# Attention heads: banded score products ahead of the third transpose group, and outputs and that group's last two transposes in PSUM banks that the exponential has left

## What is computed

```
s_loc = jnp.where(allowed, q . k_band, NEG_INF)       # window heads: a band of +-128 latents
s_ctx = q . k_context                                 # and all 256 context keys
p = sink_softmax(concat([s_loc, s_ctx]), sink)
...
s = qn . kn + qr . kr                                 # latent heads: dense over 1280 keys
p = softmax(s * MLA_SCALE);  o = p . v
```

## Time and profile before

| | |
|---|---|
| three runs | 4216.95 us median (4215.39 to 4220.05) |
| profiled execution, its own time | 4216.5 us |
| its span, first to last instruction | 4214.8 us |
| PE busy | 4039.2 us, 96% of the span |
| PEld, DVE, ACT busy | 2856.4, 1892.8, 1076.1 us |
| PE's mean granted clock | 0.981 of full speed |
| PE in the chain that ended last | 82% of the span |
| L886 (latent scores), PE | 800 instructions, 349.7 us |
| L944 and L937 (outputs), L944 on PE | 2624 instructions, 157.3 us |

### The profile page before, as it was taken

One profiled execution on the slowest core, in us unless ns is written; L12 is line 12 of the kernel. 1 busy time (PEld: TensorE's weight loads), 2 busy tenths in 40 slices (PEclk: granted clock), 3 DMA queues, 4 the chain that ended last, 5 costly groups with the idle time before them and its releaser, 6 DMA issues.

```text
span 4214.8 us, 77861 instructions
## 1 busy us (share of the span) xinstructions
PE 4039.2 (96%) x31338; PEld 2856.4 (68%) x31338; DVE 1892.8 (45%) x4216; ACT 1076.1 (26%) x2469; POOL 253.7 (6%) x254
## 2 busy tenths in 40 slices
PE   8998999999999799999999999999999987999997
PEld 4555777655544588888887555777644446999996
DVE  2235666522235443333334444666533355444446
ACT  1225666400012111111111323666400120100103
POOL 0000000000000011111111000000000000101013
PEclk9999999999999899999999999999999998999998
DMA  6111000322244798888886211000222437999996
GB/s 209 55 51 50 16 16 16 118 73 70 70 156 183 268 284 267 266 267 266 266 266 203 85 63 56 16 16 16 71 45 45 156 115 233 328 330 327 330 324 223
DMA packets 568272, 655.05 MB, mean 155 GB/s; under 512 B 20404, under 2 KB 495172, under 8 KB 568088
## 3 DMA queue, kind: packets, MB, share of 16 engines
q1 hardware_dynamic: 548024, 603.17, 44.5%
q0 software_dynamic: 19488, 47.21, 4.5%
q10 hardware_dynamic: 576, 2.10, 0.1%
HBM read 581.03 MB, written 71.39 MB: 155 GB/s over the span
## 4 chain that ended last, share of the span: by engine, by line
PE 82%; DVE 3%; DMA 2%; issue 1%; DVEq 1%; ACT 1%; SPq 1%; POOL 0%; ACTq 0%; POOLq 0%
PE PS L714 34%; PE PS L1214 9%; PE PS L1243 9%; PE PS L718 8%; PE PS L886 6%; PE PS L1053 5%; PE PS L944 3%; PE PS L937 2%; PE PS L1237 1%; PE PS L857 1%; DVE arena L1617 1%; PE PS L854 1%; PE PS L729 1%; DVE arena L2061 1%; SPq L410 1%
## 5 line engine op out<-in xcount | busy, mean ns | idle before, releaser
L714 PE MATMUL PS<-arena 128*128 128x160 f32 (+4 forms) x7200 | 1773.2, 408 | 12.9 <-DVE arena L1617 5.1
L714 PEld LDWEIGHTS PS<-arena 128*128 128x128 f32 x7200 | 1143.5, 191 | 616.3 <-issue 559.0
L1617 DVE TENSOR_TENSOR arena<-arena,PS 128x256 f32<-128x256 f32 (+3 forms) x668 | 293.6, 448 | 1056.5 <-ACT arena L1586 566.8
L1617 DVE TENSOR_TENSOR arena<-arena 128x1024 f32<-128x1024 f32 (+9 forms) x826 | 590.3, 732 | 353.9 <-PE PS L714 234.1
L718 PEld LDWEIGHTS PS<-arena 128*128 128x128 f32 (+2 forms) x3218 | 379.0, 141 | 260.6 <-issue 148.0
L718 PE MATMUL PS<-arena 128*128 128x128 f32 (+2 forms) x3218 | 490.4, 280 | 45.0 <-DVE arena L1617 16.3
L1214 PE MATMUL PS<-arena 128*64 128x128 f32 x8192 | 457.2, 274 | 3.8 <-DVE arena L1617 1.7
L1214 PEld LDWEIGHTS PS<-arena 128*64 128x64 f32 x8192 | 452.6, 138 | 8.9 <-issue 3.9
L1243 PE MATMUL PS<-arena 128*64 128x256 f32 x3584 | 396.7, 382 | 1.8 <-DVE arena L1617 1.3
L1586 ACT ACTIVATE arena<-PS 128x160 f32<-128x160 f32 (+1 forms) x256 | 74.5, 291 | 1176.1 <-PE PS L714 654.3
L1243 PEld LDWEIGHTS PS<-arena 128*64 128x64 f32 x3584 | 274.3, 138 | 119.6 <-issue 12.4
(11 more groups left out here) (218 smaller groups left out, 2256.1 us busy)
## 6 DMA issues: line engine op xcount, KB each, us to landing
arena<-in_w_exp_gate SPq DMA_DIRECT2D x128, 1024.0 KB, 6.5
arena<-in_w_exp_up SPq DMA_DIRECT2D x128, 1024.0 KB, 9.0
arena<-in_w_exp_down SPq DMA_DIRECT2D x128, 1024.0 KB, 7.7
arena<-in_w_ada SPq DMA_DIRECT2D x24, 2048.0 KB, 20.5
arena<-in_w_in SPq DMA_DIRECT2D x32, 512.0 KB, 5.4
h_transposed<-arena SPq DMA_DIRECT2D x20, 512.0 KB, 4.4
x_mid<-arena SPq DMA_DIRECT2D x18, 512.0 KB, 3.5
moe_sum<-arena SPq DMA_DIRECT2D x18, 512.0 KB, 3.5
```

Of the source, the lines that this page charges most:

```text
L714: m = pe.matmul(o, lt, rh, start=start and i == 0, stop=stop and i == n - 1)
L1617: return dve.tensor_tensor(o, x, y, op)
```

## The change

It does six things.

1. `pair` on PE issues S_A2 of `n + 1`, W0, S_A0, then S_A1, W1, W2, then `banded`, then B0, B1, B2 (S_A2 and so on being the three score products of A). Before, W1 stood ahead of S_A1 and `banded` between B1 and B2.
2. B2 goes to the third bank of the set of A of `n + 1` and waits for that exponential (`pM`, 2N + 3) in place of the copy of B0.
3. `outputs` goes to the second bank of the same set, without the wait for the copies of bank 6. The first window product has no wait left; the latent products wait for the copy of B0 at the start, for that of B1 at key block 4 and for that of B2 at key block 8.
4. A1 no longer waits for `ob`; the score product S_B1 of `n + 1`, which writes the outputs' bank, waits for it instead.
5. W2 is copied by DVE, after the maxima of A and ahead of `divisors`, and no longer by ACT ahead of the exponential of A. The counts of `pt_a` and `pt_d` follow.
6. In a context head step the window scores of `n + 1` come ahead of B, and `outputs` waits for the exponential of A of `n + 1`.

```diff
+        def out_bank(n):
+
+            return score_set("A", n + 1) + 1
+
+        def turned(part, n, ci, blocks):
+
+            b = 6 + ci % 2 if part == "W" else 7 - ci % 2
+            if part == "B" and ci == 2:
+                b = score_set("A", n + 1) + 2
+            return PS[:, b, 0:blocks * P]
+
+        ON_DVE = {"A": (0,), "W": (0, 2), "B": (0,)}
...
-                        return [lambda: None, banded] if full else [context]
+                        return [banded] if full else [context]
...
+                        if i == 1 and part == "B" and later(N):
+                            pe.wait_ge(*s("ob", N))
...
-                        if part == "A" and ci == 0:
-                            if prev:
-                                pe.wait_ge(*s("pt_a", pa_count(l, *prev, last_copy(prev[0]))))
-                        elif part == "A" and ci == 1 or part == "W" and not full:
-                            if later(N):
+                        if not full:
+                            if part == "W" and later(N):
                                 pe.wait_ge(*s("ob", N))
-                        elif not full:
+                            if part == "B":
+                                pe.wait_ge(*s("pt_a", pa_count(l, lp, n, 1)))
+                        elif (part, ci) == ("A", 2):
+                            pe.wait_ge(*s("pt_d", pd_count(l, lp, n, 1)))
+                        elif (part, ci) == ("W", 0):
                             pe.wait_ge(*s("pt_a", pa_count(l, lp, n, 1)))
-                        elif ci == 2:
-                            pe.wait_ge(*s("pt_d", pd_count(l, lp, n, "AWB".index(part) + 1)))
-                        else:
-                            pe.wait_ge(*s("pt_a", pa_count(l, lp, n, ci + (1 if part == "W" else 3))))
+                        elif (part, ci) == ("W", 1):
+                            pe.wait_ge(*s("pt_a", pa_count(l, lp, n, 2)))
+                        elif (part, ci) == ("W", 2):
+                            pe.wait_ge(*s("pt_d", pd_count(l, lp, n, 2)))
+                        elif (part, ci) == ("B", 0):
+                            pe.wait_ge(*s("pt_a", pa_count(l, lp, n, 3)))
+                        elif (part, ci) == ("B", 1):
+                            pe.wait_ge(*s("pt_d", pd_count(l, lp, n, 3)))
+                        elif (part, ci) == ("B", 2) and ahead:
+                            pe.wait_ge(*s("pM", 2 * N + 3))
...
-                    if full:
-                        pe.wait_ge(*s("pt_d", pd_count(l, lp, n, 2)))
-                        pe.wait_ge(*s("pt_a", pa_count(l, lp, n, 5)))
-                    else:
+                    o = out_bank(n)
+                    if not full:
                         pe.wait_ge(*s("pt_a", pa_count(l, lp, n, 2)))
+                        if ahead:
+                            pe.wait_ge(*s("pM", 2 * N + 3))
...
+                        pe.wait_ge(*s("pt_d", pd_count(l, lp, n, 4)))
+                    else:
+                        pe.wait_ge(*s("pt_a", pa_count(l, lp, n, 3)))
                     nm = 10 if full else 2
                     for kt in range(nm):
+                        if kt in (4, 8):
+                            pe.wait_ge(*s("pt_a", pa_count(l, lp, n, 3 + kt // 4)))
...
-                        weave(scores(p, *nx, "A") if nx else [], transposes(p, lp, n, "W"))
-                        weave(transposes(p, lp, n, "B"), scores(p, *nx, "W") if nx else [])
-                        outputs(p, lp, n)
+                        keys = scores(p, *nx, "A") if nx else []
+                        turns = transposes(p, lp, n, "W")
+                        band = scores(p, *nx, "W") if nx else []
+                        weave(keys[:2], turns[:1])
+                        for step in keys[2:] + turns[1:] + band + transposes(p, lp, n, "B", bool(nx)):
+                            step()
+                        outputs(p, lp, n, bool(nx))
...
+                        copy_chunk(p, lp, n, "W", 2)
                         divisors(p, n)
```

40 lines of the change are left out of this document (17 added, 23 removed).

## The result

The changed kernel takes 4186.86 us (median of 4 runs, 4184.61 to 4188.94); the kernel before, run beside it, 4216.17 (4 runs, 4214.59 to 4220.05). The ratio is 0.9929 with a 95% interval of 0.9917 to 0.9941: faster by 0.71%, 25 to 35 us. The direction is as predicted. The time lies 4.4 us under the predicted one and 0.14 us under the low end of the range. So the forecast was wrong, narrowly, and on the fast side.

A forecast was written before the change was run, and what follows sets the result against it. PE, busy 99% in attention, was taken as the bound. Terms 11.5 + 0.6 + 2.6 + 10.7 = 25.4 us off the profiled 4216.5 gave 4191.1, stated as 4191.3 for the median; range 4187 to 4204.

The forecast's parts named there:

- The bound and the two stalls: Attention: PE's period of 13.20 us per full head step holds two waits for ACT's copies, 0.26 and 0.12.
- second stall: Window outputs of a full head step wait for ACT to copy B1 from bank 6: 0.12 us lost, 31 heads.
- Banded products without a wait: Banded products moved ahead of B: ACT has finished the exponential of B they need, so no wait.
- refill of 0.06: Transposes of B on PE: 0.06 us extra, shown by two transposes taking 0.44 against 0.27 + 0.11.
- The tightest place, B2 behind the exponential: B2's new wait for the exponential of A: released at 614.44, wanted at 614.69, slack 0.25 us, no wait.
- The rival "slower": Exponential of A a further copy and hand-over late (0.60 + 0.20): B2 stalls, 4228 us; decides from 0.63 late; chance 0.04.
- W2's copy on DVE: W2's copy moved from ACT to DVE: takes 0.42 us, hidden by 0.9 before B1 wants it.
- Context head steps: Window scores ahead of B take 0.37 us out of the loop through `results` in seven steps: 2.6 us.
- The last head step: Last head step of a layer: B2 no longer waits for B0's copy, so outputs begin 0.6 us earlier.
- The full head steps: Attention of each layer: 0.26 us saved 30 times and 0.12 saved 31 times, 11.5 us; new period 12.82.
- first stall: B1 of a full head step waits for bank 6 until ACT's copy of W2 ends: 0.26 us, 30 per layer.
- The second merge's give-back: Second layer's merge hangs on the last `mxW`, comes 0.43 late: 10.7 us for the layer; sign: PE waiting about 1.6 longer.

The follow-up runs named there:

- banks alone: Kernel before with the changed kernel's banks and waits, but the old order of PE and W2 copied by ACT: 4202.69 us, period 13.08.
- four corners: Periods with W2 copied by ACT throughout: kernel before 13.20, only new banks 13.08, only new PE order 13.45, both 12.82 us.
- run without the drain: Changed kernel without POOL's drain between context and band key copies, and with `h_transposed` issued ahead of the merge's second weight block: 4184.59 us.
- order alone: Kernel before with only the new order of PE; banks as before, W2 copied by ACT: 4230.29 us, period 13.45.
- two copies on ACT: Changed kernel with two unread 128x128 copies put on ACT ahead of the exponential of A in full head steps: 4193.9 us.

## Why the prediction missed, point by point

- **The bound and the two stalls**: right. The period fell by 0.38, from 13.20 to 12.82, in both layers. The banks alone give the second stall's 0.12. What was wrong is how often the first one was counted (below).
- **Banded products without a wait, the refill of 0.06, S_A1 ahead of W1**: right, to 0.01. No change of tiling came with the move, and the period shows none.
- **The tightest place, B2 behind the exponential**: right that it does not bind. The slack was put at 0.25 and is 0.33; two small copies of ACT reach it. The rival "slower" decides a whole copy and hand-over further on, and nothing came near it.
- **W2's copy on DVE**: duration 0.42 said, 0.41 measured, hidden. Its return to ACT shows the same period, so the change didn't need it. (One full head step of the first layer takes 12.90 in the changed kernel and 12.82 with this copy on ACT.)
- **Context head steps**: right. The 0.37 came in each, and the run with the old context order gives 2.7 for the 2.6.
- **The last head step**: 0.63 for 0.6, in both layers.
- **The full head steps**: the first stall was counted 30 times a layer ("Per layer 30 x 0.26 + 31 x 0.12 = 11.5 us"), after the 30 waits of the earlier trace rows. Their window starts at 404, behind the first full head step, which has the stall too: its ten transposes take 1.51 at 400.97, and in the second layer at 2608.20. From 395 us on the waits view of the kernel before has 31:

```profile
PEld PS L718 <- ACT arena L1386: 8.5, 31, 0.3
```

So the term is 31 x 0.38 = 11.8 per layer and not 11.5, 0.26 short in each. The second layer shows it: it gained 12.40 by its last outputs, 11.8 and 0.63.
- **The seam** between context and full head steps had one more wait, which I did not count: A1 waited for `results` there.

```profile
396.36 0.66 PE L718 MATMUL PS<-arena 128*128 128x128 f32 x4 [0.17 <-DVE arena L1617]
```

A1 no longer waits for `ob`, and 0.16 is gained (already with the banks alone). With the 0.38 of the first full head step and 2.6 for the context this makes the 3.2 by which the time between the first outputs and those of the first full head step fell (49.92 to 46.74).
- **The second merge's give-back**: the layer gained 12.4 by its last outputs and 11.2 behind the merge's wait, so 1.2 was given back; I had 1.4 (10.7 for the layer). The wait grew by 1.12; the 1.6 that I named as a sign did not even fit my own 1.4. Right in mechanism: with the inputs issued first, the wait is gone.
- **The sum**: 27.9 in the span (27.6 in the executions' own times) against 25.4. Of the 2.5, 0.6 is in the first layer's attention (15.34 for 14.7: 0.26, 0.16 and the 0.2 of chance), 0.5 in the second (11.2 for 10.7: 0.26 and 0.2 at the merge), and the other 1.4 in stretches that the change doesn't touch (0.7 between the layers, 0.7 behind the second merge). A slip besides: 0.45 added to 4191.1 is 4191.55 and not 4191.3.
- **The step that failed.** The waits, the overlaps and the path were as predicted; sizes were not. The mis-sized term of the sum is the one of the full head steps, 11.5 per layer where 11.8 was measured; with the seam's 0.16, the merge's 0.2 and the 0.2 of chance the two attention terms were 1.1 short. That alone would have left the forecast well inside its range. The rest of the 4.4 us is what the range's low end had put too small: "the forecast's own misses (context 2.6 down, second merge not binding 1.3 up, runs 1 to 3)". It allows 1.3 for gains not seen and at most 3 for the executions. Untouched stretches gave 1.4 in the two traces, and the profiled execution of the changed kernel, 4188.94, was the slowest of its four, 2.1 above their median. Single stretches outside the attention differ by over 4 us (1777.2 to 1781.8) and over 5 (1164.0 to 1169.7) from trace to trace, and whole executions of the changed program by 4.3 and 6.7 us (4184.61 to 4188.94, 4183.16 to 4189.85); the three executions of before already lay 4.7 apart. The executions of the changed program lie on both sides of 4187. That the median fell 0.14 below it and not above is chance; that the centre was too high is not.

The prediction did not price order and banks singly. That both banks are needed once the order is changed is shown by the four corners and the two runs with one bank undone.

## What to carry to other kernels

A copy out of a PSUM bank that "costs nothing" is often hidden by the work that happens to stand between the write and the next use. A reordering that fills one stall uncovers such copies (here +0.25 instead of -0.26), and pays only together with banks that are free by then; try such parts together before judging one alone. When a stall is priced as its size times its count, count it over the whole stage: a window that starts one head step late loses one per layer. And read a forecast's range for whole time from how much the unchanged stages vary between executions, not only from the terms of the sum.

## What the runs showed of the hardware that I had not expected

**The clock after a wait.** The 4.22 us for which PE stands at the start of the second layer cost more than their length. A window of the changed kernel behind that wait, and one of the run without the drain behind its 2.55 us (columns as above; the clock is the figure before the last two):

```profile
2584.60:2586.60 2.00, 2.00 (x9) 1.70 (x8) 1.63 (x4) 0.55 (x1) 0.00 (x0) 0.50 0.00 0
```

```profile
2584.70:2586.70 2.00, 1.98 (x10) 1.35 (x11) 1.83 (x6) 1.89 (x5) 0.00 (x0) 1.00 0.00 0
```

In the changed kernel PE resumes at 2582.85 at 1.00. The granted clock is 0.79 in the microsecond from 2583, 0.50, the 1.2 GHz level, from 2584 to 2587, and 1.00 again from then on; four transposes at 2585.63 take 1.06. In the run without the drain it stays at 1.00, and they take 0.60. Of the 3.3 us that the run gained there, 2.2 came before the scores of B (8.38 and 6.21 behind the first scores), but 0.5 of these are the clock's too: the banded products take 1.77 from their start to these scores, and 1.28 in a usual head step. So about 1.6 of the 3.3 is the clock by this working, and 1.7 the wait.

How much it costs differs between executions. In the second trace of the changed kernel the clock falls while PE still waits (0.76 from 2580.40 to 2581.40, 0.50 up to 2587.40), and from the first scores to the first outputs it takes 19.75 us instead of 18.74. For the run without the drain there is one trace, so that its 2.55 us never lower the clock is not shown.

**Hand-overs.** PE follows the end of an ACT or DVE instruction by 0.05 to 0.06 us where its weight load itself waits for the counter that comes last (B2 with the order alone, with B2 in bank 7 and with two copies on ACT, and the outputs in bank 6). It follows by 0.13 to 0.15 at the outputs of the kernel before and with the order alone. There the last counter (`pt_a`) is waited for by a semaphore instruction of its own, which stands ahead of the weight load. That an instruction waits for two counters does not do it: B2 in bank 7 waits for two as well, but its semaphore instruction, for the exponential, is through at 616.19, 0.8 us ahead, and the weight load follows DVE's copy by 0.06. That the order of the two waits is the cause was not tried by itself.
